# New step orders in a streaming encoder layer, and plain fp32 products for the first block's input projection

## The reference, cut to what matters

```python
h = rmsnorm(x, norm_mix); z = h @ w_in              # 12 output tiles: us, xl, gl (4 each)
xc = causal_conv(xl); r, i = sigmoid(xc @ wa), sigmoid(xc @ wx)
a = exp(-8 r softplus(-lam)); hl = scan(a, sqrt(1-a*a) * i * xc)
y_lru = hl * gelu(gl)
ys = S5 diagonal complex state space (us), chunked; g = gelu(ys)
y_ssm = g * sigmoid(g @ w_glu)
x = x + concat(rmsnorm(y_lru), rmsnorm(y_ssm)) @ w_out
h2 = rmsnorm(x, norm_ffn); x = x + (silu(h2 @ w_gate) * (h2 @ w_up)) @ w_down   # d_ff = 2816
y = rmsnorm(x, norm_final)
```

## Time and profile before

| | us |
|---|---|
| median of 3 runs | 2579.84 (2579.05 to 2580.6) |
| profiled execution | 2573.64 |
| its span | 2571.8 |
| TensorE busy in it | 2278.7 (89%), mean granted clock 0.931 |
| VectorE busy | 1555.3 (60%) |
| ScalarE busy | 1112.3 (43%) |
| GpSimd busy | 423.0 (16%) |

### The profile page before, as it was taken

One profiled execution on the slowest core, in us unless ns is written; L12 is line 12 of the kernel. 1 busy time (PEld: TensorE's weight loads), 2 busy tenths in 40 slices (PEclk: granted clock), 3 DMA queues, 4 the chain that ended last, 5 costly groups with the idle time before them and its releaser, 6 DMA issues.

```text
span 2571.8 us, 30555 instructions
## 1 busy us (share of the span) xinstructions
PE 2278.7 (89%) x11746; PEld 2200.0 (86%) x11746; DVE 1555.3 (60%) x2601; ACT 1112.3 (43%) x1483; POOL 423.0 (16%) x483
## 2 busy tenths in 40 slices
PE   5456799989899999888999989899999888999995
PEld 4445799889799999888999889799989788999995
DVE  8665546467565656665666467565656774664544
ACT  4345434554443445444344554543445454333221
POOL 5633100023011102221010023011102221010001
PEclk9766899999899999889999999899999889999998
DMA  4373333545233554442353545233555452343331
GB/s 172 91 210 95 100 115 107 134 151 167 77 107 115 170 131 144 133 137 90 98 176 108 133 151 164 87 101 116 171 129 142 108 146 91 106 142 117 113 123 53
DMA packets 191089, 322.84 MB, mean 126 GB/s; under 512 B 82912, under 2 KB 121120, under 8 KB 190816
## 3 DMA queue, kind: packets, MB, share of 16 engines
q1 hardware_dynamic: 188576, 313.54, 40.5%
q0 software_dynamic: 2368, 7.34, 0.9%
HBM read 296.39 MB, written 26.53 MB: 126 GB/s over the span
## 4 chain that ended last, share of the span: by engine, by line
PE 79%; ACT 6%; DVE 6%; issue 4%; POOL 4%; DMA 1%; SPq 1%; POOLq 0%; DVEq 0%; ACTq 0%
PE acc L800 25%; PE acc L802 24%; PE acc L801 24%; DVE act_hl L937 2%; PE acc L866 1%; PE acc L886 1%; POOL tmp L519 1%; PE acc L876 1%; PE acc L877 1%; PE acc L856 1%; DVE rstd L1054 1%; DMA t_dram<-tq 1%; DVE w_hl L937 1%; DVE tmp L940 1%; POOL s5p L544 1%
## 5 line engine op out<-in xcount | busy, mean ns | idle before, releaser
L800 PE MATMUL acc<-act_hl,w_hl 128*128 128x416 f32 x2640 | 968.7, 367 | 61.6 <-DVE act_hl L937 61.3
L802 PE MATMUL acc<-act_hl,w_hl 128*128 128x416 f32 x2640 | 948.1, 359 | 0.0
L801 PE MATMUL acc<-act_hl,w_hl 128*128 128x416 f32 x2640 | 947.0, 359 | 0.0
L937 DVE TENSOR_TENSOR w_hl<-w_raw,w_hl 128x1024 fp32r<-128x1024 f32 x440 | 544.3, 1247 | 125.5 <-ACT w_hl L621 123.7
L800 PEld LDWEIGHTS acc<-act_hl,w_hl 128*128 128x128 f32 x2640 | 514.6, 195 | 87.3 <-DVE act_hl L937 58.7
L801 PEld LDWEIGHTS acc<-act_hl,w_hl 128*128 128x128 f32 x2640 | 514.5, 195 | 12.7 <-issue 6.6
L802 PEld LDWEIGHTS acc<-act_hl,w_hl 128*128 128x128 f32 x2640 | 512.9, 194 | 2.7
L621 ACT ACTIVATE w_hl<-w_raw 128x1024 fp32r<-128x1024 f32 x440 | 454.8, 1051 | 100.3 <-DMA w_raw<-in_w_ffn 62.0
L937 DVE TENSOR_TENSOR x_acc<-x_acc,acc 128x416 f32<-128x416 f32 x480 | 275.6, 586 | 246.7 <-PE acc L802 239.1
L519 POOL TENSOR_TENSOR tmp<-tmp 128x416 f32<-128x416 f32 x135 | 168.0, 1245 | 1218.8 <-ACT tmp L629 1209.6
L800 PE MATMUL acc<-ff_hl,w_hl 128*128 128x416 f32 x880 | 314.6, 357 | 23.4 <-DVE w_hl L937 18.4
(11 more groups left out here) (156 smaller groups left out, 1834.8 us busy)
## 6 DMA issues: line engine op xcount, KB each, us to landing
w_raw<-in_w_ffn SPq DMA_DIRECT2D x330, 512.0 KB, 3.7
w_raw<-in_w_in SPq DMA_DIRECT2D x60, 512.0 KB, 3.5
w_raw<-in_w_out SPq DMA_DIRECT2D x40, 512.0 KB, 3.3
s5y<-y_dram SPq DMA_DIRECT2D x80, 256.0 KB, 4.3
s5t<-t_dram SPq DMA_DIRECT2D x64, 162.0 KB, 4.1
s5v<-v_dram SPq DMA_DIRECT2D x80, 128.0 KB, 4.2
out_y<-x_acc SPq DMA_DIRECT2D x10, 832.0 KB, 6.4
x_acc<-in_x SPq DMA_DIRECT2D x4, 1664.0 KB, 7.6
```

Of the source, the lines that this page charges most:

```text
L800: pe.matmul(out, w(0), x(0), start=first, stop=False)
L801: pe.matmul(out, w(0), x(1), start=False, stop=False)
L802: return pe.matmul(out, w(1), x(0), start=False, stop=last)
L937: return v.tensor_tensor(out, x, y, op)
```

## The change

1. `MIXER` and `FIRST` hold new orders. Steps and counts are the same, except that the three steps `w0` (early weight splits) are gone from `FIRST`.
2. The twelve input units of block 0 (`NRAW`) are not split. VectorE writes the normalised rows to `rows`, at the memory of the first `act_hl`, and TensorE multiplies them with the raw weights: one plain fp32 product per k-tile, eight per unit instead of 24. Counts of later splits shift by `NRAW` and by KD (`split_at`).
3. `nfs` waits for its own row of the down projection, and the last block's output leaves in four stores of two rows instead of two of four.

Of the tables the start shows the form; what they do to the queues is below.

```diff
-         (28, ("cv", 0)), (28, ("xl", 1)), (28, ("zl", 0)), (28, ("ga", 0)), (28, ("gl", 0)),
-         (29, ("bx", 0)), (29, ("cv", 1)), (29, ("ga", 1)), (29, ("gl", 1)), (29, ("gl", 2)),
...
-FIRST = [("x", 0), ("pa", 0), ("sq1", 0), ("w0", 0), ("sq1", 1), ("w0", 1), ("sq1", 2), ("w0", 2), ("sq1", 3), ("tb", 0),
-         ("pq", 0), ("n1", 0), ("h1", 0), ("h1", 1), ("h1", 2), ("h1", 3),
...
@@ -109,7 +81,7 @@
     out += [("nfs", LAST, i) for i in range(4)] + [("nf", LAST, 0)]
-    out += [("y", LAST, 0), ("y", LAST, 1), ("yst", LAST, 0), ("y", LAST, 2), ("y", LAST, 3), ("yst", LAST, 1)]
+    out += [(kind, LAST, i) for i in range(4) for kind in ("y", "yst")]
     return out
@@ -124,6 +96,9 @@
 NU = len(SRC)
+NRAW = 3 * KL
+assert all(k in ("us", "xl", "gl") and not b for k, b, _ in SRC[:NRAW])
@@ -200,6 +175,8 @@
             x_acc.append(sb(f"x_acc{i}", [P, KD, T]))
+            if i == 0:
+                rows = at("rows", [P, KD, T], F32, top[0])
             act_hl.append(sb(f"act_hl{i}", [P, 2, KD, T], F32R))
@@ -315,6 +292,10 @@
+        def split_at(kind, b):
+            return h_at(kind, b) - KD
         H_PARTS = ((0, 1), (2, 3), (4, 5), (6, 7))
@@ -397,8 +378,10 @@
                 elif kind == "yst":
-                    sp.wait_ge(y_done, b * KD + 4 * j + 4)
-                    sp.dma_start(outs["y"][0][:, 4 * j:4 * j + 4, b * T:(b + 1) * T], x_acc[b % 2][:, 4 * j:4 * j + 4, :])\
+                    n = 4 if b < LAST else 2
+                    sp.wait_ge(y_done, b * KD + n * j + n)
+                    sp.dma_start(outs["y"][0][:, n * j:n * j + n, b * T:(b + 1) * T], x_acc[b % 2][:, n * j:n * j + n, :])\
                       .then_inc(y_st[b % 2], 16)
@@ -490,7 +473,7 @@
             sp.wait_ge(st_out, 48)
-            sp.wait_ge(y_st[0], 32 * 3)
+            sp.wait_ge(y_st[0], 32 * 2 + 64)
             sp.wait_ge(y_st[1], 32 * 2)
@@ -617,6 +600,8 @@
             def weight_hi(u):
+                if u < NRAW:
+                    return
                 act.wait_ge(w_in[u % RING], 16 * (u // RING + 1))
@@ -658,8 +643,6 @@
                     act.activation(pt[0][:], pt[1][:], ACT.Sin, bias=sm(HPI), scale=-1.0).then_inc(pow_done, 1)
-                elif kind == "w0":
-                    weight_hi(j)
                 elif kind == "ck":
@@ -687,9 +670,9 @@
                         act.wait_ge(x_in[b % 2], 16 * ((b + 1) // 2))
-                    if (kind, j) == ("nfs", 0):
-                        act.wait_ge(dn_free, (b + 1) * NPAIR * KD)
                     for k in (2 * j, 2 * j + 1):
+                        if kind == "nfs":
+                            act.wait_ge(dn_free, ((b + 1) * NPAIR - 1) * KD + k + 1)
                         if kind == "nls":
@@ -701,7 +684,7 @@
                             act.wait_ge(up_full, (b - 1) * NF)
-                    for k in H_PARTS[j]:
+                    for k in H_PARTS[j] if (kind, b) != ("h1", 0) else ():
                         act.wait_ge(h_made, h_at(kind, b) + k + 1)
@@ -830,8 +813,10 @@
                 kind, b, j = step
-                if step in UNIT and (kind, j % 2) != ("dn", 1):
-                    pe.wait_ge(w_lo, UNIT[step] + (2 if kind == "dn" else 1))
+                if step in UNIT and UNIT[step] < NRAW:
+                    pe.wait_ge(w_in[UNIT[step] % RING], 16 * (UNIT[step] // RING + 1))
+                elif step in UNIT and (kind, j % 2) != ("dn", 1):
+                    pe.wait_ge(w_lo, UNIT[step] - NRAW + (2 if kind == "dn" else 1))
                 if kind == "ck":
@@ -856,8 +841,16 @@
                     bank = m_bank(step)
-                    ready = (lambda k: pe.wait_ge(h_lo, h_at("h1", b) + k + 1)) if (kind, j) == ("us", 0) else None
-                    product(acc[:, bank, 0:T], UNIT[step], 0, hidden_x(b), KD, ready).then_inc(m_full, 1)
+                    if b == 0:
+                        for k in range(KD):
+                            if j == 0:
+                                pe.wait_ge(h_made, k + 1)
+                            ins = pe.matmul(acc[:, bank, 0:T], w_raw[UNIT[step] % RING][:, k * P:(k + 1) * P],
+                                            rows[:, k, :], start=k == 0, stop=k == KD - 1)
+                        ins.then_inc(m_full, 1)
+                    else:
+                        ready = (lambda k: pe.wait_ge(h_lo, split_at("h1", b) + k + 1)) if j == 0 else None
+                        product(acc[:, bank, 0:T], UNIT[step], 0, hidden_x(b), KD, ready).then_inc(m_full, 1)
                 elif kind == "ga":
@@ -903,7 +896,7 @@
                         pe.wait_ge(btT_done, 2 * KL)
-                    ready = (lambda k: pe.wait_ge(h_lo, h_at("h2", b) + k + 1)) if j == 0 else None
+                    ready = (lambda k: pe.wait_ge(h_lo, split_at("h2", b) + k + 1)) if j == 0 else None
                     product(acc[:, GATE, 0:T], UNIT[step], 0, hidden_x(b), KD, ready).then_inc(gate_full, 1)
@@ -1039,7 +1032,9 @@
             def weight_lo(u):
-                v.wait_ge(w_hi, u + 1)
+                if u < NRAW:
+                    return
+                v.wait_ge(w_hi, u - NRAW + 1)
                 slot = w_hl[u % RING]
@@ -1054,7 +1049,7 @@
             def h_lo_split(kind, b, k):
-                v.wait_ge(h_hi, h_at(kind, b) + k + 1)
+                v.wait_ge(h_hi, split_at(kind, b) + k + 1)
                 hl = act_hl[b % 2]
@@ -1126,8 +1121,6 @@
                     angles()
-                elif kind == "w0" and j < LEAD_LO:
-                    weight_lo(j)
                 elif kind == "pb":
@@ -1155,9 +1148,14 @@
                     v.wait_ge(rstd_done, n + 1)
+                    if (kind, b) == ("h1", 0):
+                        for k in H_PARTS[j]:
+                            stt(rows[:, k, :], x_acc[0][:, k, :], v1(gain + k), rstd[:], MUL, MUL)\
+                                .then_inc(h_made, 1)
+                        continue
                     for m, k in enumerate(H_PARTS[j]):
                         if k >= 2:
-                            v.wait_ge(h_lo, h_at(kind, b) + k - 1)
+                            v.wait_ge(h_lo, split_at(kind, b) + k - 1)
                         stt(tmp[:, 4 + k % 2, :], x_acc[b % 2][:, k, :], v1(gain + k), rstd[:], MUL, MUL).then_inc(h_made, 1)
```

8 lines of the change are left out of this document (2 added, 6 removed), and 20 rows, old and new, of tables (FIRST, MIXER).

## The result

| | before | after |
|---|---|---|
| median | 2580.22 us (4 runs) | 2338.51 us (4 runs, 2338.14 to 2341.01) |
| ratio | | 0.9063 (0.9048 to 0.9079) |
| profiled execution's span | 2571.8 us | 2336.3 us |
| mean granted clock of TensorE | 0.931 | 0.973 |

The account below looks back on a forecast made before the run. TensorE was taken as held by steps too close behind those they need, no engine being short overall. Terms -28 - 3 - 136 - 8 = -175 gave 2398.6, 2405 us as median; range 2360 to 2490.

Parts of the forecast that it names:

- The list of waits that go: Mixers of blocks 1 to 4: TensorE's waits named one by one as removed by the new places; 42 us to gain per stretch.
- The first block to S5: Start to first S5 product: fewer splits and earlier table sendings start S5 near 126 us instead of 154.3, -28 us.
- S5 to the first feed-forward unit: First block behind S5's start: gated unit earlier -2, plain products +2, fewer table switches -3; together -3 us.
- the tail: End of kernel: last norm's squares each wait for their own row, -8 us; four stores instead of two give 0.
- Rivals A: Mixers: the waits move to VectorE and ScalarE and half the gain per stretch is eaten; 2473 us, chance 0.22.
- B: First block: gaps keep TensorE at 1.2 GHz, plain units take 112 us, S5 starts as today; 2433 us, chance 0.10.
- C: Mixers: S5 steps wait for their whole chain, about 4.3 us each; slower, 2680 us if all sixteen, chance 0.05.
- the mixers' term: Four mixed stretches of blocks 1 to 4: 34 us gained in each, -136 us, ends -72 and -176.
- new waits: Mixed stretch: reciprocal 2 us, S5 pairs 1.34 each and 0.5, gate behind gelu 1.4, VectorE 0.8 twice; together 8.2 us.
- half clock: Mixed stretch: TensorE at reduced clock behind the new waits, some 5 us lost.
- discount for waits not found: Mixed stretch: 34 us taken of the 42 to gain, because a walk finds only waits it looks for.
- the sine's place: First block: sine ahead of the root on ScalarE lets the first table sending start near 28.5 instead of 43.75, -15 us.

Follow-up runs that it names:

- mix_only: The kernel before with the new MIXER table alone: 2382.45 us, ratio 0.9232.
- conv_late: The kernel after with each mixer's second convolution and gate step back behind the feed-forward product of place 29; first block as changed: 2359.62 us.
- out_tight: The kernel after with each mixer's gated unit, output norm, output projection and feed-forward norm back at their old, close places: 2418.07 us.
- sine_late: The kernel after with the first table round's sines and sending back behind the first norm's four row steps: 2342.48 us, ratio 0.9077.
- plain_only: The kernel before with the first block's twelve units in plain fp32, without its three early weight splits, otherwise old orders: 2562.3 us, ratio 0.9933.
- order_only: The kernel before with the new FIRST table alone, units still split and the three early weight splits kept: 2553.44 us, ratio 0.9898.

## Why the prediction was wrong

**Right.** The list of waits that go: every one went, and the table alone did it (mix_only). That the places did it is shown for the second gate step (conv_late) and for the stretch from the output norm to the split rows (out_tight), where the waits come back with the old places; for the fourth gate step, the 4.70 us of S5 step 7 and the second wait of the gated unit no run shows it. The first block to S5 (in its length; another chain ends last there), S5 to the first feed-forward unit, the tail. Rivals A, B and C did not come; TensorE's clock in the first 125 us is 0.96, and the longest wait of an S5 step for its chain is 0.34 us in the first mixer and 0.94 in the last. (Two readings were off, without weight: beside the rows there were three waits of 1 to 3 us in the stretch, not four, and the fourth stretch of 481.2 us was cut at no event, as no further mixer ends it.)

**Wrong: the mixers' term.** The mechanism was right; what failed is the price of what is left in a stretch. "Together 8.2 us, and some 5 us of half clock behind them", and then "I take 34". Step by step for the first stretch:

| | forecast | measured |
|---|---|---|
| needed without waits | 425 | 428.8 |
| new waits | 8.2 | 3.5 |
| half clock | 5 | 1.7 |
| discount for waits not found | 8 | 0 |
| length | 446 | 434.0 |

- New waits. The reciprocal was 2 against 1.68. Two pairs of S5 steps at 1.34 us each and half a microsecond for a third were priced from one pair in the earlier trace rows. In the first mixer after, S5 steps wait 0.17 and 0.34 us in all. Over the four mixers the longest such wait is 0.34 to 0.94 us (1.70 once, in mix_only). Such a pair has no fixed price. In the kernel before, two steps of another pair follow each other without a wait:

```profile
621.16 0.61 PE L886 MATMUL acc<-u,s5v 128*128 128x52 f32 x4
621.61 0.39 PE L876 MATMUL acc<-u,s5y 128*128 128x52 f32 x2
```

 The pair at 612.85 waited, it seems, because VectorE did a scan and two products (604.91 to 607.30) before the state, so that GpSimd got it late:

```profile
609.38 1.68 POOL L544 TENSOR_TENSOR s5p<-s5w,s5t 128x216 f32<-128x216 f32 x1 [13.81 <-DVE s5w L1112]
```

 The gate step behind a gelu (1.4) does not wait either, and VectorE's two small delays are 0.53 and 0.56 instead of 0.8.
- Half clock. I charged 5 us on top of 8 us of waits, as if it went with their sum. It goes with neither their sum nor simply their length: nothing behind the 1.68 us, 3.3 us of time behind the pair of S5 steps with 0.17 and 0.34. Lost are 1.7, 2.7, 1.6 and 0 us in the four mixers. Of the 46.1 us gained 28.5 are idle time (32.2 to 3.7) and 17.6 busy time, with the same products: the clock.
- The discount. "A walk finds only the waits that it looks for" was argued, not read. The walk had already counted five kinds of new wait, and all five were smaller or absent. The upper end of 44 us a stretch still left 11 of the 55 us as lost for certain, where 5.2 are, and with it the range ended above the true time.
- One stretch stood for four. From the fifth block's first gate product to the last product of the layer, 637.9 us became 580.0, 57.8 less. Some 4.3 us of it are one input unit that now stands ahead of the first gate product (the stage ahead of it grew from 153.1 to 157.4 us, 24 products more), so the last mixer gained 53.5: there the waits before were longer (5.13 and 5.07 us where the earlier trace rows have 4.04), and no half clock is left. The four gains are 46.1, 47.5, 47.0 and 53.5, 48.5 on the mean, 2.4 more than the first.

The floor, the one term that was too small (425 against 428.8), hid 3.8 us of the error a stretch. It was not the S5 steps and gates: gates, S5 steps and sums take 5.1, 20.5 and 2.1 us, 27.7 where 29 were allowed. The 2112 long products take 401 us without the half clock, where 88 units were put at 396: the first ones behind a gate step, a sum, a wait or a change of unit start 0.1 to 0.3 us late, at some 30 places.

**Right in sum, wrong in its parts.** The first block's -28 held. But the sine's place is 4 to 6 us (sine_late), not 15. The first sending came 14 us sooner through the splits that are gone (6.2 us alone, plain_only) and the order (10.5 alone, order_only: 33.23), which overlap. From S5 to the first feed-forward unit the plain units alone cost 4.2 us (plain_only, 160.2 against 156.0), where 2 were put, and the order alone won 3.3 (order_only, 152.7); with both it is 4.3 won, so these parts do not add up either, and that the -3 held is luck. At the tail the -8 held as 6.9 by the rows and 1.3 by the stores, which stood at 0. The sums of squares ended at 18.3, a gain of 3.3 of the 4 us foreseen.

## What to carry to other kernels

Price a wait by its cause (what stands before it on the engine that is late), not by the kind of step, and look for a second case of the same step without it before you charge it again. Count the half clock behind long waits apart from their idle time, and take most of it back when they go (17.6 us a stretch here, 1.7 stayed). Before a rule on the clock is drawn from one put-back wait, look whether half clock elsewhere in the stretch has gone. A discount for what a walk may have missed belongs into the range, not into the forecast.
